# A float32-grade transformer stack on one core: the first two tiles of a stage side by side, and the norm's sums from one folded block

## The reference

```
x += 0.5 * swiglu(rms(x)) ; h = rms(x) ; u = h @ w_in
x += concat(fourier(u[:512]), gqa_attention(u[512:])) @ w_out
x += 0.5 * swiglu(rms(x)) ; x = rms(x)
x += short_conv(rms(x)) ; x += mem_attention(rms(x), rms(mem)) ; x += swiglu(rms(x))
k, v = shared_kv(rms(x)) ; x += moba_attention(rms(x), k, v)
x += mem_attention(rms(x), rms(mem)) ; x += swiglu(rms(x)) ; return rms(x)
```

## Time and profile before

| | before |
|---|---|
| median of 3 runs | 1307.06 us |
| the profiled execution | 1307.18 us |
| its span | 1305.2 us |
| PE busy | 1266.6 us (97%) |
| DVE busy | 925.6 us (71%) |
| ACT busy | 664.9 us (51%) |
| POOL busy | 65.7 us (5%) |
| mean granted TensorE clock | 0.993 |

### The profile page before, as it was taken

How to read it: one execution, slowest core, us unless ns; L and a number is a source line. 1 busy time by engine, 2 the same in 40 slices (tenths; PEclk the granted TensorE clock), 3 DMA queues, 4 the chain that set the end, 5 groups by cost and what they waited for, 6 DMA issues and landing times.

```text
span 1305.2 us, 17773 instructions
## 1 busy us (share of the span) xinstructions
PE 1266.6 (97%) x7262; PEld 1106.5 (85%) x7262; DVE 925.6 (71%) x1304; ACT 664.9 (51%) x879; POOL 65.7 (5%) x41
## 2 busy tenths in 40 slices
PE   8999999998999999999999999999889999999997
PEld 7888887877888887888888888888778888888886
DVE  6777857566777854887658777669877656777743
ACT  6665544365555544455546555454455445555532
POOL 1000000001000000341001000010001001000000
PEclk9999999999999999999999999999999999999998
DMA  8565653123555663455336555644335444455550
GB/s 305 177 218 184 224 193 124 71 98 129 180 183 189 204 217 125 161 194 193 130 129 226 181 184 185 225 161 143 132 116 191 148 144 161 165 191 194 193 194 33
DMA packets 51297, 221.73 MB, mean 170 GB/s; under 512 B 4336, under 2 KB 5648, under 8 KB 30736
## 3 DMA queue, kind: packets, MB, share of 16 engines
q1 hardware_dynamic: 50496, 219.47, 48.3%
q10 hardware_dynamic: 720, 1.12, 0.3%
HBM read 219.52 MB, written 1.05 MB: 169 GB/s over the span
## 4 chain that ended last, share of the span: by engine, by line
PE 82%; DVE 13%; ACT 2%; issue 2%; DMA 1%; POOL 1%; SPq 0%; DVEq 0%; ACTq 0%
PE bank L390 47%; PE bank L394 25%; DVE wt L1021 3%; PE bank L429 2%; PE bank L633 2%; PE bank L465 2%; PE bank L432 1%; PE bank L594 1%; ACT scratch L854 1%; DMA raw<-weights 1%; DVE scratch L1105 0%; DVE work L1201 0%; DVE scratch L1234 0%; DVE x L1035 0%; PE bank L615 0%
## 5 line engine op out<-in xcount | busy, mean ns | idle before, releaser
L1021 DVE TENSOR_TENSOR wt<-raw,wt 128x2048 fp32r<-128x2048 f32 x202 | 462.3, 2292 | 70.2 <-ACT wt L750 69.9
L390 PE MATMUL bank<-xn,wt 128*128 128x512 f32 x1856 | 454.6, 394 | 5.3 <-DVE xn L1030 4.7
L750 ACT ACTIVATE wt<-raw 128x2048 fp32r<-128x2048 f32 x202 | 386.1, 1912 | 116.3 <-PE bank L394 102.5
L390 PEld LDWEIGHTS bank<-xn,wt 128*128 128x128 f32 x1856 | 339.7, 189 | 74.0 <-DVE xn L1030 8.7
L390 PE MATMUL bank<-h,wt 128*128 128x512 f32 (+1 forms) x1088 | 270.0, 395 | 1.9 <-DVE h L1422 0.9
L394 PEld LDWEIGHTS bank<-xn,wt 128*128 128x128 f32 x1856 | 240.3, 192 | 10.2
L394 PE MATMUL bank<-xn,wt 128*128 128x256 f32 x1856 | 243.1, 283 | 0.0
L390 PEld LDWEIGHTS bank<-h,wt 128*128 128x128 f32 (+1 forms) x1088 | 198.2, 189 | 43.9 <-issue 3.6
L394 PEld LDWEIGHTS bank<-h,wt 128*128 128x128 f32 (+1 forms) x1088 | 143.3, 191 | 11.0 <-issue 2.6
L394 PE MATMUL bank<-h,wt 128*128 128x256 f32 (+1 forms) x1088 | 148.6, 284 | 0.0
L762 ACT ACTIVATE rest<-bank 128x512 f32<-128x512 f32 x129 | 76.6, 594 | 116.2 <-PE bank L394 116.1
(11 more groups left out here) (170 smaller groups left out, 862.4 us busy)
## 6 DMA issues: line engine op xcount, KB each, us to landing
raw<-weights SPq DMA_DIRECT2D x158, 1024.0 KB, 4.9
raw<-weights SPq DMA_DIRECT2D x92, 512.0 KB, 5.2
k_t<-mem_t SPq DMA_DIRECT2D x2, 1024.0 KB, 8.1
raw<-weights SPq DMA_DIRECT2D x4, 256.0 KB, 7.3
x<-x_t ACTq DMA_DIRECT2D x4, 256.0 KB, 6.8
out_t<-work SPq DMA_DIRECT2D x4, 256.0 KB, 2.3
v_s<-fourier SPq DMA_DIRECT2D x2, 256.0 KB, 5.3
con<-consts SPq DMA_DIRECT2D x1, 385.5 KB, 9.6
```

What stands on the lines that cost most here:

```text
L390: return pe.matmul(out, hi, a.rearrange("p a s -> p (a s)"), start=first, stop=False, skip_group_check=True)
L750: act.activation(wt[t % RING][:, 0], raw[t % RING][:], ACT.Copy).then_inc(weight_hi, 1)
L1021: dve.tensor_tensor(wt[t % RING][:, 1], raw[t % RING][:], wt[t % RING][:, 0].bitcast(F32), ALU.subtract).then_inc(weight_lo, 1)
```

## The change

The change has six parts. In gu1, gu2, gu3 and conv_out the first two tiles run side by side: blocks 0 to 5 of both, then blocks 6 and 7 of both. The output projections w_out, mem_o0, moba_o, mem_o1 use pairs A, B, C, A, and the other pairs are shifted to fit. POOL also folds pair 3 and then one half on the other, so PE sums one block instead of four. The sums stand before block 5 of tile 1 (before block 7 of tile 1 in the gate stages), and the gate stages' factors before block 7 of tile 2; the conv stage's two spreads move to tiles 2 and 3. A gate tile's banks are free when it has been taken out ("taken"), ahead of the multiplication by the factors. The second memory attention begins with the memory value tile, with four tiles ahead instead of three. The loads of x go through SP's queue, between the pieces of the first tile.

```diff
-MEM1 = [("q", 0), ("q", 1), ("v", 0), ("k", 2), ("q", 2), ("k", 3), ("q", 3), ("v", 1), ("v", 2), ("v", 3)]
+MEM1 = [("v", 0), ("q", 0), ("q", 1), ("k", 2), ("q", 2), ("k", 3), ("q", 3), ("v", 1), ("v", 2), ("v", 3)]
...
-    ("w_in", [B, C, A, B, A]), ("gqa", [A, B, A, B]), ("w_out", [A, B, A, B]),
-    ("gu1", [A, C, B] * 7 + [A]), ("down1", [C, B, DD, A]),
-    ("conv_in", [C, B, A] * 4), ("conv_out", [C, B, A, C]),
-    ("mem0", [B, A, C, B] + [A, B] * 2), ("mem_o0", [A, B, A, B]),
+    ("w_in", [B, C, A, B, A]), ("gqa", [A, B, A, B]), ("w_out", [A, B, C, A]),
+    ("gu1", [B, C, A] * 7 + [B]), ("down1", [C, A, DD, B]),
+    ("conv_in", [C, A, B] * 4), ("conv_out", [C, A, B, C]),
+    ("mem0", [A, B, C, A] + [B, A] * 2), ("mem_o0", [B, A, C, B]),
...
+            if _name.startswith("gu"):
+                _taken += 1
+                TAKEN[_name, _j] = _taken
+                _emptied[_p] = ("taken", _taken)
...
-AHEAD = {"gqa": 1, "mem0": 4, "moba": 5, "mem1": 3}
+AHEAD = {"gqa": 1, "mem0": 4, "moba": 5, "mem1": 4}
...
             for b in range(KP):
                 sp.dma_start(rows_of(raw[0][:], 2 * b, 2 * b + 2), ...)
+                sp.dma_start(x[:, pair(b), :], x_t[:, pair(b), :]).then_inc(x_landed[b], 16)
...
-                for b in (1, 2):
+                for b in range(1, KP):
                     pool.wait_ge(squared, KP * SUM[name] + b + 1)
...
+                pool.wait_ge(folded, KP * i + KP - 1)
+                pool.tensor_tensor(work[:, 0, :], work[:, 0, :], work[:, 1, :], ALU.add).then_inc(folded, 1)
...
-                blocks = [0, 1, 6, 7] if name in FOLD else list(range(KB))
+                blocks = [0] if name in FOLD else list(range(KB))
...
-                    return {1: {1: lambda: sums(name)}}
-                return {1: {1: lambda: sums(name)}, 2: {1: lambda: spread_factor(name)}}
+                    return {1: {5: lambda: sums(name)}}
+                return {1: {5: lambda: sums(name)}, 2: {1: lambda: spread_factor(name)}}
+
+            def two_tiles(t, outs, a, ready, beside):
+                for ks in ((0, 6), (6, KB)):
+                    square_tile(t, outs[0], a, ready=ready, ks=ks)
+                    square_tile(t + 1, outs[1], a, ks=ks, beside=beside)
...
+                if n:
+                    two_tiles(t0, [banks_for(phase, j) for j in range(2)], xn, operand(name), {7: lambda: sums(name)})
+                for j in range(2 if n else 0, FF):
...
+                                beside=norm(name, True).get(j, {}) if n == 0 else {7: lambda: spread_factor(name)} if j == 2 else {},
...
-                            beside={1: {5: lambda: spread_factor("mix0")}, 2: {5: lambda: spread_diagonal(DIAG["mix0 first"], 0)}}.get(j, {}))
+                            beside={2: {1: lambda: spread_factor("mix0")}, 3: {1: lambda: spread_diagonal(DIAG["mix0 first"], 0)}}.get(j, {}))
...
-            residual("conv_out", lambda k: [(y_split, k // 2 + 1)])
+            for ks in ((0, 6), (6, KB)):
+                for b in range(2):
+                    residual("conv_out", lambda k: [(y_split, k // 2 + 1)], b, b + 1, ks)
+            residual("conv_out", None, 2)
...
-            for b in range(KP):
-                act.dma_start(x[:, pair(b), :], x_t[:, pair(b), :]).then_inc(x_landed[b], 16)
...
+                def scaled_tile(j):
+                    whole_of(phase, j, gu_s[j % 3], taken)
+                    factored(j)
+
+                def factored(j):
+                    dve.wait_ge(taken, TAKEN[phase, j])
+                    dve.tensor_tensor(gu_s[j % 3], gu_s[j % 3], both(r_x[:]), ALU.mult).then_inc(drained, 1)
...
                 if n:
                     after(t0)
-                factors(name, col_x)
-                after(t0 + 1)
-                spread_to(name, r_x)
+                    whole_of(phase, 0, gu_s[0], taken)
+                    factors(name, col_x)
+                    spread_to(name, r_x)
+                    factored(0)
+                    after(t0 + 1)
+                else:
+                    factors(name, col_x)
+                    after(t0 + 1)
+                    spread_to(name, r_x)
+                    scaled_tile(0)
...
             after(FIRST["conv_in"])
+            whole_of("conv_in", 0, conv_s[0], drained)
             dve.wait_ge(spread, DIAG["mix0"])
```

More of the change, by code:

```diff
@@ L96 @@
              7: ([], [(13, 4, 8), (O0, 0, 3)], [(O0, 3, 7)])},
-    "mem1": {0: ([(3, 0, 8), (4, 0, 8), (5, 0, 2)], [(5, 2, 8), (6, 0, 8)]), 1: ([], [(7, 0, 8), (8, 0, 3)]),
+    "mem1": {0: ([(4, 0, 8), (5, 0, 2)], [(5, 2, 8), (6, 0, 8)]), 1: ([], [(7, 0, 8), (8, 0, 3)]),
              2: ([], [(8, 3, 8), (9, 0, 4)]), 3: ([(9, 4, 8)], [(O0, 0, 6)], [(O1, 0, 6)])},
@@ L249, in program @@
         tile_done = sem("tile_done")
-        rest_copied, drained = sem("rest_copied"), sem("drained")
+        taken, rest_copied, drained = sem("taken"), sem("rest_copied"), sem("drained")
         acc_done = sem("acc_done")
@@ L271, in program @@
         out_gained, out_ready, stored = sem("out_gained"), sem("out_ready"), sem("stored")
-        EMPTIES = {"added": added, "drained": drained}
+        EMPTIES = {"added": added, "drained": drained, "taken": taken}
         CONST_DMAS = 2 * 16
@@ L455, in sums @@
                 at = acc[0] if name == "final" else stat
-                blocks = [0, 1, 6, 7] if name in FOLD else list(range(KB))
+                blocks = [0] if name in FOLD else list(range(KB))
                 if name in FOLD:
-                    pe.wait_ge(folded, 2 * (FOLD[name] + 1))
+                    pe.wait_ge(folded, KP * (FOLD[name] + 1))
                 for k in blocks[slice(*ks) if ks else slice(None)]:
-                    if name not in FOLD and k % 2 == 0 or k == 6:
+                    if name not in FOLD and k % 2 == 0:
                         pe.wait_ge(squared, KP * SUM[name] + k // 2 + 1)
@@ L465, in sums @@
                         mm = pe.matmul(at[:, 0, cols * n:cols * (n + 1)], work[:, k, n * P:(n + 1) * P],
-                                       weigh[:, k, 0:cols], start=k == 0 and n == 0, stop=k == KB - 1, skip_group_check=True)
+                                       weigh[:, k, 0:cols], start=k == 0 and n == 0, stop=k == blocks[-1], skip_group_check=True)
                 if not ks or ks[1] == len(blocks):
@@ L488, in gate_up @@
                 t0 = FIRST[phase]
-                for j in range(FF):
+                if n:
+                    two_tiles(t0, [banks_for(phase, j) for j in range(2)], xn, operand(name), {7: lambda: sums(name)})
+                for j in range(2 if n else 0, FF):
                     ready = operand(name) if j == 0 else None
@@ L497, in gate_up @@
                     square_tile(t0 + j, banks_for(phase, j), xn, ready=ready, in_parts=in_parts,
-                                beside=norm(name, n == 0).get(j, {}), ms=1 if j == FF - 1 and n < 2 else 2,
+                                beside=norm(name, True).get(j, {}) if n == 0 else {7: lambda: spread_factor(name)} if j == 2 else {},
+                                ms=1 if j == FF - 1 and n < 2 else 2,
                                 cuts=((2, 4, 6) if j == 0 else (4,)) if in_parts else (6,) if j == 0 else ())
@@ L1122, in scaled_halves @@
                     sum_s = rest_s[i % 3][:, 0, :]
-                    link(dve.tensor_tensor(sum_s, pair_banks(phase, j)[:, 0, 0:S], sum_s, ALU.add))
+                    dve.tensor_tensor(sum_s, pair_banks(phase, j)[:, 0, 0:S], sum_s, ALU.add).then_inc(taken, 1)
+                    dve.wait_ge(taken, TAKEN[phase, j])
                     for m in range(2):
@@ L1147, in gate_up @@
                         scaled_halves(j)
-                    else:
-                        scaled(phase, j, gu_s[j % 3], r_x[:])
+                    elif j:
+                        scaled_tile(j)
                     if j == 0 or j > 2:
@@ L1400, in _ @@
                         dve.wait_ge(y_split, p)
-                    whole_of("conv_in", j, conv_s[0], drained)
+                    if j:
+                        whole_of("conv_in", j, conv_s[0], drained)
                     dve.wait_ge(drained, ROT["conv_in"] + j + 1)
```

9 lines of the change are left out of this document (5 added, 4 removed).

## The result

The changed kernel takes 1300.52 us (median of 5 runs, 1299.26 to 1301.76), against 1307.06 (1306.59 to 1307.54): a ratio of 0.9948, 95% interval 0.9935 to 0.9961. That is faster, as forecast, but the time lies 1 us above the range of 1290.3 to 1299.5 and 6.0 us above the forecast. The profiled execution took 1301.76 us, its span is 1300.0.

The account below looks back on a forecast made before the run. It took PE, busy 97% of the span, as the bound. Terms 8.96 + 0.44 - 0.6 + 1.20 + 0.63 + 0.60 + 1.3 gave 12.5 us off 1307.18, stated as 1294.5 us; 8-in-10 range 1290.3 to 1299.5.

Parts of the forecast that it names:

- conv: Conv stage: later spread and tiles side by side gain 0.60 us of the 2.5 its two waits cost; bounds 0.3 to 2.5.
- one queue: Start: x's loads alternating with weight pieces on SP's queue gain 1.3 us; bounds -1.0 and 2.3.
- Sums from one block: Nine folded norms: PE sums 4 records instead of 16, saving 1.28 us each; seven give it whole, 8.96 us.
- I price the wait for POOL at nothing: Folded norms: POOL's sum is ready before PE asks, so no cost; without that cover up to 1 us a norm.
- w_in and moba: DVE is behind the sum: w_in meets the same chain and gains 0.44 us; moba loses 0.6, bounds -1.3 to 0.
- Output projections: w_out, mem_o0 and mem_o1: new bank pairs remove waits, 1.20 us together; w_out 0.66 of at most 0.74.
- tiles side by side: Gate stages: worth nothing by itself, the 0.46 us wait before block 4 stays; worth something in conv_out.
- mem1: Second memory attention: beginning with a tile that needs no x removes the wait at its beginning, 0.63 us.
- rival 4: Gate stages: DVE's backlog never drains, its loop exceeding PE's tile; slower than before, 1310 at a 5.85 us loop; chance 0.04.
- the slacks of 0.4 and 0.55: Gate stages: diagonal ready 0.4 us early, tile 5's split 0.55 early; no cost, or 0.5 us per stage if failing.
- Rival 2: Start: gives nothing or loses 1 us, all else holds: 1296 to 1297 us; chance 0.10.
- Rival 1: Gate stages, moba, mem0: diagonal or splits late, or POOL's folds late or slowing DVE: 1299 us; chance 0.18.

Follow-up runs that it names:

- e7: Changed kernel with mem's squares at gate tile 10 instead of 3 and mix0's 32 sums in two halves beside blocks 1 and 3: 1300.87 us, ratio 0.9945.
- e13: e8 with conv_in's beginning as before the change (mix0's factor spread at block 5 of the second tile): 1295.43 us, ratio 0.9909.
- e3: Changed kernel with mem's squares, and so POOL's folds of them, at gate tile 10 instead of 3: 1299.59 us, ratio 0.9933.
- e6: Kernel before with only x's loads moved to SP's queue, between the weight pieces: 1308.77 against 1308.73 us, ratio 0.9999.
- e1: The changed kernel run again without edit: 1301.65 us against 1308.65 for the kernel before, ratio 0.9949.
- e8: Changed kernel with mem's squares at gate tile 10, mix's and mix1's norms as before, and x0's sums later: 1297.62 us, ratio 0.9916.
- e5: The kernel before, unaltered, run once for a second profile: 1309.66 us.
- e9: e8 with mix0's 32 sums in two halves, beside blocks 1 and 7 of conv_in's second tile, and a later spread: 1299.05 us, ratio 0.9927.
- e10: e8 with mix0's 32 sums in quarters, beside blocks 1, 3, 5 and 7 of conv_in's second tile, and a later spread: 1298.84 us, ratio 0.9931.

## Why the prediction was wrong, point by point

**The bookkeeping.** Fifteen profiles more made the table above readable. Each of its stretches repeats to about 0.1 us between runs of the same order (gqa and w_out to 0.3), with three exceptions: the start, head sums to gqa (17.7, 19.2 or 20.7 us) and conv. Here is conv_in to mem0 by what the clock did at mix0's sums:

| | stays up | half for 3.4 us | half for 6.8 us |
|---|---|---|---|
| before (3 profiles) | 96.56 | 96.54 | 97.66 |
| new order (9, and e7) | 96.38 (2 of 9) | 97.95 (7 of 9) | 99.59 (e7) |
| e13 | | 96.15 | |

With the clock alike, start and head sums at no gain and conv at 0.18, the measured gains of the first table sum to 8.95. From there: conv costs on average (2 x 96.38 + 7 x 97.95)/9 = 97.60 against 96.92, 0.86 us worse than that 0.18; from head sums to gqa the five profiles of the new w_in average 19.25 against 18.19 in the twelve of the old one, 1.06; the start is 0.2 later. That makes 6.8 us, where medians gave 6.5 and 7.0 and ratios 6.7 to 6.8.

So 5.7 of the forecast's 12.5 us are missing. By terms of its sum: one queue, 1.5 (1.3 of gain that did not come, and 0.2 of loss); x0's sums and mem's folds, 2.1; conv, 1.3 (0.60 forecast, -0.68 measured); the head sums' stretch, 1.06 where the forecast had 0; moba, 0.6. The other rows together gave 0.8 more than forecast.

**Sums from one block: right for the sums of six norms, wrong for x0's place and for mem's folds.** mem's, ffn2's, mem0's, ffn0's, mem1's and ffn1's sums gave the 1.28 of the forecast; the stretches without another term gained 1.3 to 1.4, and gu1's gained 1.03 because PE came to it sooner than DVE (below). The step that failed is "I price the wait for POOL at nothing": its cover was worked out for w_in, the gate stages and the memory attentions, and not for x0's sums, which stand in the first stage's tile 1 right behind the start. Beside it a step was missing: what a fold costs DVE, which I had weighed only in moba. x0's sums waited 0.70 (0.86 by starts) for the half fold and its stretch gained 0.4 (e3), and mem's folds took 1.25 from PE through DVE's split at 47.92: 2.1 us less than forecast. I had used for POOL's side, 2.61 beside DVE, and outside moba never asked what DVE pays.

The Trainium skill, "SBUF — State Buffer", section "Who interferes with whom", has DVE instructions with two inputs in SBUF contend with GpSimd's reads under an exclusive lock. The traces agree: DVE's split takes 3.38 when a fold is already running and 2.28 alone, and moba's four rests take 3.19 beside two folds and 2.12 beside one.

**One queue: wrong, 1.3 us.** I counted loads in a queue (2/7 of 8.09) as if each took the same share of time. e6 says 0.9999. In the first profile of the changed kernel the third piece of weights, on which the chain had hung, did land sooner, at 9.06 instead of 10.17 us. But x's last pair landed at 12.62 instead of 11.08, and the chain went over to it: my term followed one load, and not the last one that is needed before tile 1. The Trainium skill, "DMA: Bandwidth & Descriptors", section "Issuing engines are not separate DMA queues", says that another issuer saves issue time only; I had quoted it against my term and kept the term. The measurement sides with the page.

**w_in and moba: right in mechanism up to the head sums.** T to the head sums gained 0.48 (0.44). The wait there grew to 2.48 (2.5). What failed is the 0 behind it: "PE saves 1.28 but meets the same chain" seems to have a price. At this wait and its narrow matmuls the clock falls in all 17 profiles, for 3.4 us where the stretch takes 17.7, for 6.8 where it takes 19.2 or 19.3 and for 10.2 in e1, where it takes 20.7. It is down for longer than 3.4 in four profiles of five with the long wait, against four of twelve with the wait of 1.70. That the longer wait is the cause is suggested by these counts and not shown. Moba lost 1.20, near the end of the stated bounds: the forecast's own 0.55, and by difference 0.65 for DVE's rests and split beside folds. e8 takes back both at once (1.21), so it does not tell them apart.

**Conv: wrong sign.** I had the new wait for tile 5's split nearly right (1.34 by starts; I had 1.11), and 0.18 of gain with full clock instead of 0.60. But the old wait for the diagonal, 1.21 us, was a cushion, and conv_out's wait behind it another: in e6 a half clock of 3.4 us shrank the first to 0.40 and the second from 0.90 to 0.44, and cost nothing (96.54 against 96.56). The late spread took the first cushion away, and the half clock, which came in seven of nine profiles, is then paid in full, 1.57. e13, with the spread back in its place, does not pay. I read one profile, in which the half clock had not come.

**Output projections, tiles side by side, mem1: right, and too low.** 1.14 for 0.66 in w_out, 2.54 for 2.18 in mem1 and mem_o1: by starts PE stood longer at the banks than its idle 0.81 shows (1.08). But 0.34 of w_out's gain comes back as gu1's longer wait, because DVE cannot follow: the net, 0.80, is close to the 0.74 that I had worked out as all that DVE allows. No new wait in the gate stages: rival 4 is refuted, and the slacks of 0.4 and 0.55 held.

**The rivals and the range.** Rival 2, the start that gives nothing, came true (1.5 us for about 2.0). Rival 1 named POOL's late folds and their slowing of DVE, and both came, but not where it put them: 3 of its 4.5 us were for new waits in three gate stages, which did not come, while gu0, which it did not name, lost 2.1. Added up, the two prices give 1301.0, near the measured time; that is luck, since the 1.9 us that the clock took (0.86 in conv, 1.06 behind the head sums) are in neither. The range let only one rival happen at a time and had nothing for the clock.

## What to carry to other kernels

An instruction moved to an idle engine is not free if its operands share a path with a busy one: price the neighbour's instructions too, and put such work where that neighbour has slack (tile 10 instead of tile 3: 1.25 us). Before you remove a wait, ask what else it absorbs. And read more than one profile of the kernel before: from the head sums to gqa the one I had took 17.7 us, the next two with the old w_in 19.2 (e5) and 19.3 (e6), and the clock behind mix0's sums had not fallen in it at all, as it did in ten of thirteen.

## What the runs showed of the hardware that was not expected

TensorE's granted clock falls to 1.2 GHz in the midst of a kernel that keeps it 97% busy. It does so at two kinds of place. One is the row of 32 narrow matmuls in conv_in (3.6 us), with no wait of 1 us ahead of it: within or behind it in ten profiles of thirteen. Behind a group of 16 narrow ones (1.70 us) that stands alone it falls in no profile. The other is a wait of PE's: at the 1.7 or 2.5 us before the head sums in all 17 profiles, at a wait of 3.0 in gqa in all 17, at conv_in's new wait of 2.55 in both that have it (e9, e10), and at moba's wait of 3.1 in two of six (e1, e7). Narrow matmuls are not needed there: in e1 and e10 the clock falls before the first matmul behind the wait, and in e9 wide ones follow. It comes by chance: the first profile of the kernel before has none in moba, the sixteen others one or two.

Each fall lasts 3.4 or 6.8 us, once 10.2 (the end of the kernel aside). Where PE sets the time, as behind the 32 sums of the new order, 3.4 us at half cost 1.57, and 6.8 us cost 3.2 (e7). Where a wait follows that can shrink, it costs less or nothing: moba and moba_o take 131.7 to 131.8 us in the first profile of the kernel before, in e5 and in e6, with no fall, two and one. The falls are the main part of the spread between those three: e5 takes 2.5 us more than the first and e6 1.5 more, and of this the head sums' stretch and conv give 2.7 and 1.6.
